# Half-height array tiles and rounded bias tables in a two-block transformer's fourth mixer, and one score product moved up

## The reference, cut to what matters

```python
# first mixer (mLSTM): a projection to 4 input and 4 forget gates per token
gates = tok[..., o4:].astype(f32) + gate_b.astype(f32)
# third mixer (latent attention): each of 8 heads has a 64-wide and a 32-wide rotary part
s = (einsum('bhqd,bhkd->bhqk', qn, k_nope) + einsum('bhqr,bkr->bhqk', qr, k_rope)) * scale
# fourth mixer (odd_mixer): one projection, two kinds of attention, one output projection
cq, ck, cv, sq, sk, sv = split_cols(h @ w_in, ODD_SPLITS)
o_dil = dilated_attention(groups(cq), groups(ck), groups(cv), slopes)   # 3 groups x 4 heads of 64
o_sb = stick_breaking_attention(sq, sk, sv)                             # 4 heads of 64
return concatenate([heads_last(o_dil), heads_last(o_sb)]) @ w_out
```

## Time and profile before

| | us |
|---|---|
| median of 3 runs | 1743.17 (1740.46 to 1749.1) |
| the profiled execution, its device time | 1745.23 |
| its span in the trace | 1743.4 |
| TensorE matmul busy | 1673.4 (96%) |
| TensorE weight load busy | 1493.2 (86%) |
| VectorE busy | 1229.3 (71%) |
| ScalarE busy | 947.0 (54%) |
| GpSimd busy | 10.7 (1%) |
| granted TensorE clock, mean | 0.992 of 2.4 GHz |

### The profile page before, as it was taken

How to read it: one execution, slowest core, us unless ns; L and a number is a source line. 1 busy time by engine, 2 the same in 40 slices (tenths; PEclk the granted TensorE clock), 3 DMA queues, 4 the chain that set the end, 5 groups by cost and what they waited for, 6 DMA issues and landing times.

```text
span 1743.4 us, 29020 instructions
## 1 busy us (share of the span) xinstructions
PE 1673.4 (96%) x10776; PEld 1493.2 (86%) x10776; DVE 1229.3 (71%) x2010; ACT 947.0 (54%) x1634; POOL 10.7 (1%) x18
## 2 busy tenths in 40 slices
PE   7999999899999999998999999989999998989997
PEld 7888897798888888886888889878999897789986
DVE  6777656677777777776677776767787666578775
ACT  6555453555555555557565554366665442456653
POOL 1000000000000000000000000000000000000000
PEclk9999999999999999999999999999999999999999
DMA  7554553265546544541355456215544643134442
GB/s 293 183 192 153 206 197 120 75 211 188 185 149 220 190 176 157 196 170 71 112 192 191 155 180 241 98 42 189 182 172 153 217 177 120 56 138 173 174 162 95
DMA packets 47648, 285.54 MB, mean 164 GB/s; under 512 B 5900, under 2 KB 6668, under 8 KB 24512
## 3 DMA queue, kind: packets, MB, share of 16 engines
q1 hardware_dynamic: 45216, 278.94, 45.2%
q10 hardware_dynamic: 1952, 4.60, 0.7%
q0 software_dynamic: 384, 0.68, 0.1%
HBM read 283.15 MB, written 1.05 MB: 163 GB/s over the span
## 4 chain that ended last, share of the span: by engine, by line
PE 88%; DVE 6%; ACT 4%; issue 1%; DMA 0%; ACTq 0%; SPq 0%; DVEq 0%
PE ps_gemm L175 33%; PE ps_gemm L182 31%; PE ps_gemm L183 16%; DVE s_wlo L90 2%; ACT s_whi L81 1%; PE ps_s L910 1%; PE ps_gemm L910 1%; ACT s_work L958 1%; PE ps_gemm L936 1%; PE ps_sum L223 1%; DMA s_wraw<-in_stream_dram 0%; PE ps_sum L863 0%; PE ps_gemm L1389 0%; PE ps_s L907 0%; PE ps_gemm L926 0%
## 5 line engine op out<-in xcount | busy, mean ns | idle before, releaser
L90 DVE TENSOR_TENSOR s_wlo<-s_wraw,s_whi 128x1024 fp32r<-128x1024 f32 (+3 forms) x602 | 622.9, 1076 | 383.1 <-ACT s_whi L81 383.1
L81 ACT ACTIVATE s_whi<-s_wraw 128x1024 fp32r<-128x1024 f32 (+3 forms) x600 | 531.9, 934 | 408.4 <-PE ps_gemm L183 207.2
L182 PE MATMUL ps_gemm<-s_xr,s_whi 128*128 128x512 f32 x1408 | 496.5, 397 | 1.1 <-DVE s_work L637 1.1
L183 PE MATMUL ps_gemm<-s_xr,s_wlo 128*128 128x256 f32 x1408 | 395.0, 281 | 0.0
L175 PE MATMUL ps_gemm<-s_xr,s_whi 128*128 128x256 f32 x2128 | 387.8, 285 | 5.2 <-DVE spare_lo L806 1.8
L182 PE MATMUL ps_gemm<-hid_r,s_whi 128*128 128x512 f32 x1056 | 370.9, 394 | 2.9 <-DVE hid_r L600 2.9
L175 PEld LDWEIGHTS ps_gemm<-s_xr,s_whi 128*128 128x128 f32 x2128 | 332.3, 192 | 10.4 <-issue 6.1
L182 PEld LDWEIGHTS ps_gemm<-s_xr,s_whi 128*128 128x128 f32 x1408 | 264.2, 188 | 65.9 <-issue 1.7
L175 PE MATMUL ps_gemm<-s_xr,s_wlo 128*128 128x256 f32 x1064 | 301.0, 283 | 0.0
L183 PE MATMUL ps_gemm<-hid_r,s_wlo 128*128 128x256 f32 x1056 | 294.7, 279 | 0.0
L183 PEld LDWEIGHTS ps_gemm<-s_xr,s_wlo 128*128 128x128 f32 x1408 | 266.0, 189 | 0.1
(11 more groups left out here) (383 smaller groups left out, 1517.5 us busy)
## 6 DMA issues: line engine op xcount, KB each, us to landing
s_wraw<-in_stream_dram SPq DMA_DIRECT2D x177, 1024.0 KB, 4.8
s_wraw<-in_stream_dram SPq DMA_DIRECT2D x96, 704.0 KB, 4.0
s_wraw<-in_stream_dram SPq DMA_DIRECT2D x16, 768.0 KB, 4.3
s_wraw<-in_stream_dram SPq DMA_DIRECT2D x16, 512.0 KB, 3.3
s_room<-in_o_bias_dram ACTq DMA_DIRECT2D x1, 1536.0 KB, 8.9
s_room<-in_mem_dram SPq DMA_DIRECT2D x4, 256.0 KB, 6.1
s_x<-in_x_dram SPq DMA_DIRECT2D x1, 1024.0 KB, 11.5
s_room<-in_e_alibi_dram ACTq DMA_DIRECT2D x1, 1024.0 KB, 5.8
```

Source lines behind the costliest of these rows:

```text
L81: c.act.activation(c.whi[:, slot, s], c.wraw[:, raw, s], ACT.Copy).then_inc(c.hi_ready, 1)
L90: last = c.dve.tensor_tensor(c.wlo[:, slot, s], c.wraw[:, raw, s], c.whi[:, slot, s].bitcast(F32), ALU.subtract)
L182: pe.matmul(bank, w_hi, x_both, start=k == 0, stop=False)
L183: return pe.matmul(left, w_lo, x_hi, start=False, stop=k == ks - 1)
```

## The change: 64-partition and 32-column tiles, bias in two rounded parts, one job's scores earlier

Heads are packed two to a tile of 128 partitions, without zeros, and products contract over 64 partitions (lower for one head, upper for the next, into different banks). In the dilated jobs of the first query block the middle group's heads lie swapped; their two products come after a wait on a new semaphore (rows_done) that TensorE signals to itself. In the jobs of the second block the order is group 0 (first bank), group 1 (second bank, other half), group 2 (first bank, first half again). The bias table is split on the host into a high and a low part, loaded as one table of 128x6144 (3 MB; before, two tables of 2.25 MB together), copied to fp32r by ScalarE in four copies of 1536 columns between the splits, and multiplied with a rounded identity matrix. The stick-breaking scores use ps_s and two ps_gemm banks (before: three ps_gemm banks). The first dilated job's scores go ahead of the stick-breaking values on TensorE, and its maximum ahead of L2591 on VectorE. The gate products alternate between partitions 0 to 3 and 32 to 35. The rotary products of the latent jobs contract over 64 partitions. The weight columns are permuted on the host to match. The diff, cut to its core (o.k shrinks from 12 to 6 tiles, o.sk from 4 to 2; the bookkeeping of bank counts follows):

```diff
@@ scores_pe @@
-    for first, ident, bias in job.bias:
+    for first, ident, bias, fresh in job.bias:
         cols = bias.shape[1] if len(bias.shape) == 2 else bias.shape[1] * bias.shape[2]
         out = bank[:, first:first + cols]
         if len(bias.shape) == 3:
             out = out.rearrange("p (h w) -> p h w", w=bias.shape[2])
-        c.pe.matmul(out, ident, bias, start=True, stop=False, skip_group_check=True)
+        c.pe.matmul(out, ident, bias, start=fresh, stop=False, skip_group_check=True)
     for first, width, pairs in job.scores:
         for a, (q, k) in enumerate(pairs):
             last = c.pe.matmul(bank[:, first:first + width], q, k, start=a == 0 and not job.bias, stop=a == len(pairs) - 1,
                                skip_group_check=bool(job.bias))
+    if job.swapped:
+        last.then_inc(c.rows_done, 1)
+        c.pe.wait_ge(c.rows_done, job.swapped[0])
+        for first, width, q, k in job.swapped[1]:
+            last = c.pe.matmul(bank[:, first:first + width], q, k, start=False, stop=True, skip_group_check=True)
@@ exps_act, maxima_dve @@
-        last = c.act.activation(c.ss[:, s, h * w:(h + 1) * w], bank[:, h * w:(h + 1) * w], ACT.Exp,
...
-    dve_step(c, cnt, dve.tensor_reduce(m, bank[:, 0:job.cols].rearrange("p (h w) -> p h w", w=job.width), AX, ALU.max))
+    heads = bank[:, 0:h * job.stride].rearrange("p (h w) -> p h w", w=job.stride)[:, :, 0:job.width]
+    dve_step(c, cnt, dve.tensor_reduce(m, heads, AX, ALU.max))
@@ mix_a_pe @@
-    for side in range(2):
-        for k in range(KD):
-            last = pe.matmul(gates[0:4, side * T:(side + 1) * T], c.w_gate[:, k, 4 * side:4 * side + 4], c.xn[:, k, :],
-                             start=k == 0, stop=k == KD - 1)
+    for k in range(KD):
+        for side in range(2):
+            last = pe.matmul(gates[32 * side:32 * side + 4, side * T:(side + 1) * T], c.w_gate[:, k, 4 * side:4 * side + 4],
+                             c.xn[:, k, :], start=k == 0, stop=k == KD - 1)
@@ mix_a_dve @@
-    dve.tensor_tensor(a.z[0:4, :], bank[0:4, T:2 * T], c.inv[0:4, :], ALU.mult).then_inc(c.bank_free, 4)
+    dve.tensor_tensor(a.z[0:4, :], bank[32:36, T:2 * T], c.inv[32:36, :], ALU.mult).then_inc(c.bank_free, 4)
@@ latent_jobs @@
-            scores = [(place[h] * w, w, [(e.qr[:, h // 4, q], e.kr[:, h % 4, 0:w])]) for h in place]
+            turned = {h: slice(h % 2 * B_HD, (h % 2 + 1) * B_HD) for h in place}
+            scores = [(place[h] * w, w, [(e.qr[turned[h], h // 4, q], e.kr[turned[h], E_GROUP[h % 4], 0:w])]) for h in place]
@@ dilated_jobs @@
-            table, b0 = o.bias1 if blk else o.bias0, j0 * 3 * w
-            bias = [(i, c.ident[:, :], table[:, b0 + i:b0 + min(i + BANK, 6 * P)]) for i in range(0, 6 * P, BANK)]
-            scores = [(((j - j0) * 3 + g) * w, w, [(o.q[:, 2 * g + j // 2, q], o.k[:, 4 * g + j, 0:w])])
-                      for j in range(j0, j0 + heads) for g in range(3)]
+            if blk:
+                pieces = [(0, j0, slice(0, 2)), (BANK, j0, slice(2, 3))]
+            else:
+                pieces = [(0, j0, slice(0, 3)), (BANK, j0 + 1, slice(0, 3))]
+            bias = [(first, c.ident_r[:, :], o.bias_r[:, part, j, gs, T - w:T], part == 0)
+                    for first, j, gs in pieces for part in range(2)]
+            place = lambda g, j: ((j - j0) * BANK + O_PLACE[g] * w, w)
+            heads_ = lambda g, j: (o.q[dilated_rows(g, j), 2 * g + j // 2, q], o.k[dilated_rows(g, j), 2 * g + j // 2, 0:w])
+            scores = [(*place(g, j), [heads_(g, j)]) for g in ((0, 1, 2) if blk else (0, 2)) for j in range(j0, j0 + heads)]
+            swapped = () if blk else (j0 // 2 + 1, [(*place(1, j), *heads_(1, j)) for j in range(j0, j0 + heads)])
@@ mix_o_pe @@
-            for side in range(2):
-                bank = next_bank(c, cnt)
-                for j in (2 * side, 2 * side + 1):
-                    last = pe.matmul(bank[:, j % 2 * T:(j % 2 + 1) * T], o.sk[:, j, 0:P], o.q[:, 6 + j // 2, :], start=True, stop=True)
-            bank = next_bank(c, cnt)
-            for j in range(4):
-                last = pe.matmul(bank[:, j * P:(j + 1) * P], o.sk[:, j, P:T], o.q[:, 6 + j // 2, P:T], start=True, stop=True)
+            pe.wait_ge(c.exp_ready, cnt.job)
+            banks = [c.ps_s[:, 0:BANK], c.ps_s[:, BANK:2 * BANK], next_bank(c, cnt), next_bank(c, cnt)]
+            for first in (0, P):
+                for j in range(4):
+                    rows, w = slice(j % 2 * B_HD, (j % 2 + 1) * B_HD), T - first
+                    out = banks[2 * (first // P) + j % 2][:, j // 2 * w:(j // 2 + 1) * w]
+                    last = pe.matmul(out, o.sk[rows, j // 2, first:first + P], o.q[rows, 6 + j // 2, first:T],
+                                     start=True, stop=True)
...
+    jobs = dilated_jobs(c, o)
+    pe.wait_ge(c.rounded, 4 + 4)
+    scores_pe(c, jobs[0], cnt.job, c.ps_s)
     pe.wait_ge(c.bank_free, cnt.out)
     pe.wait_ge(c.o_probs_ready, 1)
...
     pe.wait_ge(c.inv_columns, cnt.columns)
-    jobs = dilated_jobs(c, o)
-    pe.wait_ge(c.o_tables_in, 32)
-    first_scores_pe(c, cnt, jobs)
+    pe.wait_ge(c.bank_free, cnt.out)
+    scores_pe(c, jobs[1], cnt.job + 1, c.score_banks[1])
@@ mix_o_act @@
-    for dst, name in ((o.bias0, "o_bias0"), (o.bias1, "o_bias1")):
-        act.dma_start(dst, c.dram[name]).then_inc(c.o_tables_in, 16)
+    act.dma_start(o.bias, c.dram["o_bias"]).then_inc(c.o_tables_in, 16)
...
-    split_for(split_hi, c, cnt, u0 + 8)
-    act.wait_ge(c.bank_free, g0 + 14)
+    act.wait_ge(c.o_tables_in, 16)
+    flat = o.bias_r.rearrange("p s j g t -> p (s j g t)")
+    for part in range(4):
+        split_for(split_hi, c, cnt, u0 + 5 + part)
+        s = slice(part * 6 * T, (part + 1) * 6 * T)
+        rounded_act_copy(c, flat[:, s], o.bias[:, s])
+    act.wait_ge(c.bank_free, g0 + 13)
@@ mix_o_dve @@
-    def keys(i, dst, h):
-
-        split_for(split_lo, c, cnt, u0 + i)
-        dve.wait_ge(c.unit_done, u0 + i + 1)
-        bank = bank_of(c, cnt.out)
-        for r in range(2):
-            rows = slice(r * B_HD, (r + 1) * B_HD)
-            last = dve.tensor_tensor(dst[rows, h + r:h + 4:2, :], bank[rows, :].rearrange("p (k t) -> p k t", t=T),
-                                     c.inv[rows, :].unsqueeze(1).to_broadcast([B_HD, 2, T]), ALU.mult)
-        last.then_inc(c.bank_free, 1)
-        cnt.out += 1
+    def keys(i, g):
+        take(c, cnt, u0 + i, pair(o.k, g), slice(0, 2 * T))
...
-    for i in range(3):
-        dve.tensor_scalar(o.z[:, i * 2 * T:(i + 1) * 2 * T], bank_of(c, cnt.out), B_HD ** -0.5, None,
+    dve.tensor_scalar(o.z[:, 0:4 * T], c.ps_s[:, :], B_HD ** -0.5, None, ALU.mult).then_inc(c.o_z_taken, 1)
+    for first in (4 * T, 5 * T):
+        dve.tensor_scalar(o.z[:, first:first + T], bank_of(c, cnt.out)[:, 0:T], B_HD ** -0.5, None,
                           ALU.mult).then_inc(c.bank_free, 1)
         cnt.out += 1
+    dve.wait_ge(c.o_z_taken, 1)
...
+    jobs = dilated_jobs(c, o)
+    maxima_dve(c, cnt, jobs[0], cnt.job, c.ps_s)
...
-    attention_dve(c, cnt, dilated_jobs(c, o), lambda i: split_for(split_lo, c, cnt, u0 + 11))
+    attention_dve(c, cnt, jobs, lambda i: split_for(split_lo, c, cnt, u0 + 11), None, 1)
@@ tables @@
-    out["o_bias1"] = bias.reshape(P, -1)
-    out["o_bias0"] = bias[..., P:].reshape(P, -1)
+    bias = np.stack([bias[:, :, O_PLACE.index(i)] for i in range(3)], axis=2).astype(np.float32).reshape(P, -1)
+    m, e = np.frexp(bias)
+    high = np.ldexp(np.round(m * 2 ** 12) / 2 ** 12, e).astype(np.float32)
+    out["o_bias"] = np.concatenate([high, bias - high], axis=1)
@@ program @@
-            zero_keys(c, "mix_o", (views["mix_o"].sk, views["mix_o"].k))
```

51 lines of the change are left out of this document (31 added, 20 removed).

## The result

The changed kernel took 1728.97 us in the median of 5 runs (1728.21 to 1731.76), the kernel before, beside it, 1744.31 (1740.46 to 1749.1). The ratio is 0.9909, with a 95% interval of 0.9893 to 0.9924. The forecast was 1727.3 us, in a range of 1722 to 1736, from a sum of 15.9 us; the medians differ by 15.3. The profiled execution of the changed kernel took 1728.21 us with a span of 1726.4 (before 1743.4), at a mean granted clock of 0.990.

What follows compares the result with a forecast made beforehand. TensorE was taken to bound the kernel (88% of the chain). Gains of 3.4 + 2.9 + 3.0 + 0.7 + 5.9 = 15.9 us took the profiled 1745.23 to 1729.3, as a median 1727.3 us; range 1722 to 1736.

Steps and rivals of the forecast that it cites:

- Gates: First mixer: the 16 gate products, 7.00 us before, overlap fully in 8 pairs; gain 3.4 us.
- Rotary products: Third mixer: each of three latent jobs' rotary products goes from 1.82 us to 0.86; gain 2.9 us.
- Stick-breaking scores: Fourth mixer: unit 3 gets a bank read long before and eight products become four pairs; gain 3.0 us.
- Keys: Key units written in one VectorE instruction, 0.68 us instead of 1.39; one of four on the path; gain 0.7 us.
- Copies: ScalarE's four rounding copies, 1.47 us each, fit into its idle time between splits; cost 0.
- Dilated jobs: Fourth mixer's dilated jobs: shorter bias and scores, job 0 started earlier; gain 5.9 us, bounds 3 and 6.9.
- The walk: Step-by-step timing of dilated jobs 0 to 5: last scores end at 1499.0 instead of 1504.88.
- a new wait of 0.5: Dilated jobs: TensorE waits 0.5 us before turn(0), as VectorE has job 1's maximum ahead of divide(0).
- Latency: Rival: dilated jobs become bound by their way over VectorE and ScalarE; gain there 3, total 1730.2 us; chance 0.14.
- the products would not overlap: Rival: none of the new pairs overlap; gains only 6.4 us, total 1736.8 us; chance 0.05.
- slower case: Rival: every tile step drains the array at 0.2 us and nothing overlaps; 6.4 us slower, 1749.6 us; chance 0.04.
- The clock rival: Rival: TensorE's clock drops once more or once less, 1.4 us either way, 1728.7 or 1725.9 us; chance 0.06.

Runs made afterwards that it cites:

- the rotary experiment: Changed kernel with the third mixer's rotary products contracting over 128 partitions again, zeros included; 1730.91 us.
- The bank experiment: Kernel before, its stick-breaking scores moved to two ps_s banks and one ps_gemm bank, still products over 128 partitions; 1748.04 us.
- the last experiment: Changed kernel profiled once more without an edit; span 4.5 us longer than its first profile; median of 6 runs on the same chip 1730.99 us.

## Why the prediction was right, point by point

1. *Gates, forecast 3.4, measured 3.1.* Full overlap of four-partition outputs, taken from rows of 64-partition outputs, was right: 16 products in 3.56 us. The Trainium skill's share of 2.38 in 3 ("TensorE: Matmul & The Clock Gate", "Measured speedup vs the span model") would have given 2.6 and does not show here: two column tiles gave 7.00 / 3.56 = 1.97. The term missed 0.3 us because the read by VectorE, of which the forecast said "this read just stays hidden", does not stay so: its L806 ended at 269.17, and its two gate reads at 270.40, 0.24 us after the scores (268.51 + 1.65). VectorE was as late as forecast (5.45 us after the gates' start, forecast 5.4); it was the scores that the forecast took too long, at 1.9 us instead of the 1.65 from their start to the next product.
2. *Rotary products, forecast 2.9, measured 2.3 in this pair of profiles, 1.5 to 2.9 over all.* The products were as forecast (job: 1.93 us for rotary and nope together). What was mis-sized is what lies around them: 0.64 instead of 0.55 us from the bias to the products, since the change of shape now comes there (0.54 again in the rotary experiment), and in this profile a wait of 0.34 us for VectorE (L1033) before the second job. In the two profiles with neither that wait nor a clock drop the same stretch gained 2.5 us. The forecast did not reckon with clock drops inside this stretch.
3. *Stick-breaking scores, forecast 3.0, measured 3.02.* The bank experiment splits it: 1.99 for the wait, 1.03 for the tiles. The forecast's 1.75 for the wait was 0.24 too little and the 1.3 that it left for the tiles about as much too high: the total is right in part by luck.
4. *Keys, forecast 0.7, measured 0.94.* From unit 6's keys to the next step VectorE needs 0.60 us (1437.19 to 1437.79) instead of 1.43 (1448.19 to 1449.62), 0.83 less where the forecast took the difference of the durations, 0.71; the last 0.11 lie in the split ahead of it. No run undid the keys alone.
5. *Copies, forecast 0.* Two experiments bear it out: without them, and with twice as many, the stretch from the stick-breaking scores to job 0 stays within 0.04 us.
6. *Dilated jobs, forecast 5.9, measured 5.8.* The walk holds step by step, with small errors that cancel: bias 0.87 us instead of 0.76 (0.12 for entry was too little), scores 1.06 as forecast, job 0 2.01 instead of 1.97, wait of turn(0) 0.37 instead of 0.5, period 3.63 instead of 3.6. The parts, each by undoing it: the rounded bias 3.1 us, job 0's place 1.8; the half-height scores are left with about 1 if the parts simply add, which was not tried by itself.

The forecast of "a new wait of 0.5" is in VectorE's timeline, the maximum of job 1 ahead of divide(0):

```profile
1475.11 0.96 DVE L996 TENSOR_REDUCE s_small<-ps_gemm 128x2 f32<-128x768 f32 x1 [2.33 <-PE ps_gemm L917]
...
1476.37 0.96 DVE L1029 TENSOR_TENSOR s_work<-s_work,s_small 128x768 f32<-128x768 f32 x1
```

**The rivals.** Latency did not take over: from job 3 on, no wait stands between the jobs. That the products would not overlap, or each drain the array, fell with the gates (3.56 us) and the scores (1.51 us). For outputs of four partitions too, changing only the tile cost nothing (32 records in 16 steps of 0.216 us and 0.1 around them): by the rule that the Trainium skill gives in "TensorEngine Tiling (Array Packing)", "Key Properties", which the prediction set against its slower case, the runs agree. The clock rival was real, and the argument against it was wrong: "TensorE keeps its 1.00 here" holds for most executions, but in two of the seven profiles with this order of jobs the clock fell in the middle of the dilated jobs, which cost 1.1 us, behind a wait of 1.50 us, no longer than those of the kernel before; and in six of ten it fell in the first latent job.

**Where the sum could have misled.** The forecast's sum was 15.9, the touched places give 15.2, and the medians differ by 15.3. That these agree so well is in part luck. In the second profile of the changed kernel the clock fell in the first latent job (11.59 instead of 10.30 us) and in the dilated jobs (20.71 instead of 19.61), and the same places give 15.2 - 1.3 - 1.1 = 12.8 us.

The spans of the two single profiles differ by 17.0. Divided where the feed-forward stages (L182) begin and end, the parts with the first, third and fourth mixer differ by 4.8, 2.8 and 9.8 us. The first is 3.1 for the gates and 1.7 for a clock drop that only the kernel before had there (0.66 over 290 to 295 us); the third has 0.5 us outside the stretch counted above; the fourth is what its places give. The rest nearly cancels: the feed-forward stages were 4.2 us faster in the changed kernel's profile (one 2.1 slower, the next two 4.2 and 2.0 faster, by the two paces of the last experiment), and the parts that are left, before, between and behind them, 4.6 us slower, where clock drops took part of it back.

## What to carry to other kernels

Plain fp32 products that use half of the array's rows, or four of its columns, ran two at a time here where the tiles differ and the order brings them within two products of each other; strict alternation is not needed, but runs of eight on one tile kept only a quarter of the gain (6.14 us, between 7.00 and 3.56). The shortest idle time of an engine among its steps (2.35 us) is only a lower bound: elsewhere 3.8 us were free, and two copies fitted. Where whole runs of a kernel spread more than an edit is worth, read the edit's own stretch; here the total pointed the wrong way for two edits of ten.
